# The last weight transfer of a mixer and mixture-of-experts block, divided by partitions

## The reference, cut to what matters

```python
x = x + mixed @ w_o                          # the two gated mixers, before the experts
h = rms_norm(x, norm_ffn)
combine = top_2_of_the_best_group(h)         # (256, 32), two weights per row, the rest zero
for e in range(32):
    a = silu(h @ w_gate[e]) * (h @ w_up[e])  # w_gate, w_up: (1024, 512) for each expert
    x = x + combine[:, e:e + 1] * (a @ w_down[e])   # w_down: (512, 1024)
out = rms_norm(x, norm_final)
```

## Time and profile before

| what | value |
|---|---|
| median of 3 runs | 729.03 us (728.8 to 730.17) |
| profiled execution, its own time | 728.23 us |
| its span, first to last instruction | 726.3 us |
| mean granted TensorE clock | 0.893 of full speed |
| mean rate of all transfers over the span | 334 GB/s |
| last unit (half 1): from its issue to its landing | 19.34 us |
| last unit: size | 1024 KB |

### The profile page before, as it was taken

The page is one execution under the profiler, slowest core; times in us unless marked ns, Lnnn a source line. Parts: engine busy times, 40 slices in busy tenths (PEclk is TensorE's granted clock), DMA queues, the critical chain, the costliest instruction groups (busy, mean ns, idle before and its releaser), DMA issues.

```text
span 726.3 us, 7579 instructions
## 1 busy us (share of the span) xinstructions
PE 554.2 (76%) x3257; PEld 331.3 (46%) x3257; DVE 204.1 (28%) x432; ACT 72.6 (10%) x139; POOL 43.9 (6%) x68
## 2 busy tenths in 40 slices
PE   6999999999999998998384594566448347457765
PEld 6888888888886656354041141123114113112411
DVE  3898979897012144000010000000001001000002
ACT  3101020202100013100000000000000000000002
POOL 5001212212000011000000000000000000000000
PEclk9999999999999999999696788779679669778988
DMA  9992812445495648899999999999999999999993
GB/s 248 390 304 83 292 56 71 161 157 192 144 406 232 231 174 319 354 431 428 427 426 430 428 426 430 429 427 426 431 425 427 430 429 427 427 429 426 424 406 152
DMA packets 46097, 242.43 MB, mean 334 GB/s; under 512 B 9618, under 2 KB 9710, under 8 KB 35822
## 3 DMA queue, kind: packets, MB, share of 16 engines
q1 hardware_dynamic: 45198, 238.77, 81.2%
q10 hardware_dynamic: 864, 3.15, 1.3%
HBM read 240.86 MB, written 1.05 MB: 333 GB/s over the span
## 4 chain that ended last, share of the span: by engine, by line
PE 52%; DMA 42%; DVE 2%; SPq 2%; issue 2%; ACT 0%; POOL 0%; DVEq 0%; PEldq 0%; POOLq 0%; ACTq 0%
PE bank L1150 29%; DMA ring<-in_w_down 15%; DMA ring<-in_w_gate 13%; PE bank L1389 8%; DMA s_region<-in_w_up 4%; DMA x_region<-in_w_up 4%; PE bank L1397 4%; DMA ring<-in_w_up 4%; PE bank L1271 4%; PE bank L1438 2%; DMA ring<-in_w_in 1%; SPq L471 1%; PE bank L1356 1%; PE bank L1243 1%; PE bank L1258 1%
## 5 line engine op out<-in xcount | busy, mean ns | idle before, releaser
L1389 PE MATMUL bank<-ring,z_region 128*32 128x512 f32 x688 | 116.3, 668 | 64.0 <-DMA ring<-in_w_gate 14.9
L1150 PE MATMUL bank<-x_region,ring 128*128 128x256 f32 x688 | 152.9, 381 | 0.0
L1150 PEld LDWEIGHTS bank<-x_region,ring 128*128 128x128 f32 x688 | 129.3, 190 | 22.5 <-issue 4.3
L1389 PEld LDWEIGHTS bank<-ring,z_region 128*32 128x32 f32 x688 | 32.8, 121 | 123.5 <-issue 123.5
L1397 PE MATMUL bank<-ring,m_region 128*32 128x512 f32 x240 | 55.4, 737 | 27.8 <-DMA ring<-in_w_down 16.6
L1063 DVE TENSOR_TENSOR z_region<-z_region,bank 128x512 f32<-128x512 f32 x8 | 8.2, 1027 | 209.3 <-PE bank L1389 197.2
L1389 PE MATMUL bank<-x_region,z_region 128*32 128x512 f32 x80 | 43.7, 708 | 11.0 <-DMA ring<-in_w_up 11.0
L1067 DVE COPY m_region<-bank 128x512 f32<-128x512 f32 x8 | 5.5, 692 | 141.7 <-PE bank L1397 113.6
L1397 PE MATMUL bank<-s_region,m_region 128*32 128x512 f32 x64 | 37.3, 750 | 9.0 <-DMA ring<-in_w_down 9.0
L1389 PE MATMUL bank<-rot_region,z_region 128*32 128x512 f32 x64 | 36.0, 727 | 8.4 <-DMA ring<-in_w_up 8.4
L1356 PE MATMUL bank<-conv_region,h_region 128*128 128x128 f32 x256 | 33.2, 285 | 4.7 <-issue 4.1
(11 more groups left out here) (244 smaller groups left out, 551.7 us busy)
## 6 DMA issues: line engine op xcount, KB each, us to landing
ring<-in_w_gate SPq DMA_DIRECT2D x29, 2048.0 KB, 34.5
ring<-in_w_up SPq DMA_DIRECT2D x20, 2048.0 KB, 32.4
ring<-in_w_down SPq DMA_DIRECT2D x20, 2048.0 KB, 35.2
ring<-in_w_in SPq DMA_DIRECT2D x11, 2048.0 KB, 10.3
s_region<-in_w_up SPq DMA_DIRECT2D x4, 2048.0 KB, 34.5
rot_region<-in_w_down SPq DMA_DIRECT2D x4, 2048.0 KB, 32.6
s_region<-in_w_down SPq DMA_DIRECT2D x4, 2048.0 KB, 35.9
x_region<-in_w_up SPq DMA_DIRECT2D x4, 2048.0 KB, 37.0
```

Source lines behind the costliest of these rows:

```text
L1150: ins = MM(dst, w[:, k, n * P:(n + 1) * P], rhs[:, k, :], start=k == 0, stop=k == kn - 1)
L1389: ins = MM(bank[to][quarter(e), :], xT[:, k, quarter(e)], of_expert[e][:, FF * k:FF * k + FF], start=k == 0, stop=k == KD - 1)
```

## The change

The last unit is issued as 16 DMAs. Each of them moves the 4 pieces of 2 KB for 8 neighbouring partitions, 64 KB in all. They go out one after the other on the SP queue and raise the same semaphore, so TensorE waits for 15 x 16 more. The other units are issued as before. The bytes, their source and their destination are the same.

```diff
+STRIP = 8
...
-                sp.dma_start(dst[:, 0:e * n].rearrange("p (e n) -> p e n", e=e), src).then_inc(landed, 16)
+                if v < len(UNITS) - 1:
+                    sp.dma_start(dst[:, 0:e * n].rearrange("p (e n) -> p e n", e=e), src).then_inc(landed, 16)
+                    return
+                for p in range(0, P, STRIP):
+                    sp.dma_start(dst[p:p + STRIP, 0:e * n].rearrange("p (e n) -> p e n", e=e),
+                                 src[p:p + STRIP]).then_inc(landed, 16)
...
                 uses = transfers_to(slot, range(MIX_UNITS)) + sum(slot_of(w) == slot for w in range(v + 1))
+                if v == len(UNITS) - 1:
+                    uses += P // STRIP - 1
                 pe.wait_ge(slots[slot][1], uses * 16)
```

## The result

The changed kernel takes 734.52 us (median of 9, 731.51 to 736.38) against 729.07 us (9 runs) for the kernel before: a ratio of 1.0073, 95% interval 1.0056 to 1.0090. It is slower by 5.4 us, and its times scatter over 4.9 us where these nine of the kernel before lie within 1.6 us (in a later set of 23 the kernel before scatters over 4.3 us, with one time above 731). The profiled execution took 732.92 us, 1.6 us less than the median, with a span of 730.8 us, 4.5 us longer than before.

The account below looks back on a forecast made before the run. The weights' arrival by DMA was taken to bound the kernel. Eight engines carrying the last unit (2.53 us) plus completions (0.1) made 2.63 us, added to 729.03 for 731.7 us, range 728.7 to 736.5.

Parts of the forecast that it names:

- the count of completions: Last unit's DMAs: completions rise from 16 to 128, small packets by 112; cost taken 0.1 us, at most 0.3.
- the mechanism that I called the likeliest: Last unit runs on eight engines, some of them late, with no slowdown between neighbouring partitions: 731.7 us, chance 0.36.
- my own signs of being wrong: Profile after: 16 completions per small transfer, rate below 150 GB/s, last landing still 715.7, or line 1479's matmuls at half clock.
- the blocking rival: Last unit: engines writing neighbouring partitions share a way into SBUF; 5.1 to 7.6 us more, 734.5 (732 to 740), chance 0.30.
- The end follows the data: End of kernel: each microsecond the last unit lands later adds one to the span; landing earlier gains 0.25 us at most.
- Half 0: Unit ahead of the divided one: goes first in every engine's queue, so its matmuls still start at 712.60 us.
- Eight engines: Last unit: a transfer of 8 partitions runs on eight engines, all 16 on the same eight; 5.07 us at 207 GB/s.
- A late engine among the eight, 2.53 us: Last unit: the eight engines used include some that finish late, so the end moves by 2.53 us; lower bound nothing.
- No blocking between neighbours: Last unit: engines writing neighbouring partitions do not slow each other; cost taken as nothing.
- Sixteen issues cost nothing: SP queue: 16 issues take 5.0 to 8.8 us, done by 710.2, needed about 717; cost nothing, cover 7 us.
- Slow sequence of small transfers: Last unit: the 16 transfers come out one per 1.5 us, ending 10 us late; 739 us, chance 0.07.
- TensorE's clock: TensorE at the end: a 2.9 us wait is too short to lower its clock; cost nothing, at most 1.5 us.

Follow-up runs that it names:

- warm matmuls: Against the changed kernel, unused matmuls added before TensorE's waits for half 0 (8) and for the copy of half 0 (2): 734.22 us, ratio 1.0064.

## Why the prediction was right, and where it was not

The direction, the range (728.7 to 736.5) and the count of completions were right. The point, 731.7 us, was 2.8 us too low, and the mechanism that I called the likeliest is only a part of what the runs show. Two of my own signs of being wrong came true: the rate fell below 150 GB/s (143 from 714 to 716 us), and half 1's matmuls ran in part at half clock (1.57 us against 1.07). The range held the result because it took in most of the blocking rival.

- *The end follows the data.* Right, but in the profile after the chain goes through half 0, which I had left where it was: "Half 0. It goes before the strips in every engine's queue; its matmuls start at 712.60 and should stay there." This is the step that failed. It holds for one engine's queue; between engines, an early engine's transfers slowed an earlier unit of a late one. Measured: half 0's matmuls start 3.36 us later, 1.83 of them spent waiting for data where it was 0.70 before. With 32 neighbours even the unit ahead of half 0 was waited for by 4.03 us.
- *Eight engines.* Shown by 112 more small packets.
- *A late engine among the eight, 2.53 us.* I took this against the bound of nothing, and it held. With partitions 4 apart the last 2 KB packet ends at 717.34 us against 714.85 before, 2.5 us later, with two engines' 49 GB/s at the end. Some six of the eight are early (60 completions against 18 between 708 and 711 us), and their share fell into their idle time, but the end follows the last engine. What was missing is what comes on top: in the changed kernel the last 2 KB packet ends at 718.85 us, 4.0 us later than before, and at 720.26 us in the profile with warm matmuls, 5.4 us later.
- *No blocking between neighbours.* I took the value nothing and priced blocking as a rival at 734.5 with a chance of 0.30. The measured median is 734.52, and 63 GB/s for 8 neighbours against 160 for partitions 4 apart, alone, shows that the grouping of partitions makes such transfers slow. That the price fits to 0.02 us is luck: the rival counted only a longer transfer of the divided unit, by 5.1 to 7.6 us, and neither half 0's delay nor the clock was in it. The rule in the Trainium skill, SBUF — State Buffer, section "Door 1: The DMA port swizzle", holds here in its form: spans of 8, 16, 32 and 64 neighbours moved 63, 121, 212 and 210 GB/s, and by its table they reach 2, 4, 8 and 8 ports. The last pair, the same rate for twice the partitions, is its most particular claim. An estimate from its 27.2 GB/s per port is 54 for 8 neighbours, where 63 were measured; transfers that follow each other reach different ports, and some overlap of them may be the reason. This agreement, and no run, is what puts the blocking on the side of SBUF and not of HBM. The late engines' slower packets while the strips went into low partitions are not explained by it.
- *Sixteen issues cost nothing.* Right for neighbours: 0.30 us each where SP did not wait for room, and the last went out at 708.12 us. With a step the issues take 0.68 us.
- *Slow sequence of small transfers.* Ruled out as the main cause: 8 transfers of 16 and 4 of 32 lose as much as 16 of 8, 2 of 64 lose 4.5 us, and 4 of 128 lose nothing.
- *TensorE's clock.* I took nothing, because the wait would be shorter than the 4.5 us of the earlier trace rows, and named 1.5 us as the most. That inference failed: TensorE waited 1.83 us, ran the matmuls of half 0, waited 0.72 us, and had half clock (0.50) from 717.7 on. The first addition took 2.08 us instead of 1.13; the extra between the two matmul groups is 1.14 us in all. Keeping the clock up in one place gave back nothing that could be told from the scatter, so its share is not settled.

Three things stay open. By what way the late engines are slowed from the first strip on. Why 32 neighbours are the slowest, when alone they move more than 8 or 16 do: its profile shows a wait of 4.03 us for the unit ahead of half 0, but not why that unit is held back more. And why the changed kernel scatters over 4.9 us: the lag between early and late engines when the divided unit comes up may differ between executions, which no run isolates. No divided version beat the kernel before. The transfers of all 128 partitions equal it, and it has only the 0.25 us that TensorE waited to give.

## What to carry to other kernels

If a load has to be divided, divide it along the free dimension and let each transfer span all 128 partitions (729.12 us here, no loss). Every division by partitions made the kernel slower, and alone, runs of 8, 16 and 32 neighbours moved 63, 121 and 212 GB/s. A DMA share near 1 is no proof of a full rate: read the GB/s beside it. And when transfers of different shapes follow each other on a queue, ask what the engines that are ahead do to those that are behind: the unit that is late can be one in front of the one you changed.

## What the runs showed of the hardware that I had not expected

- With one transfer shape per run and nothing beside it, 2.1 MB in 4 KB pieces moved at 350 to 362 GB/s into 128 partitions, 210 to 212 into 64 or 32 neighbours, 121 into 16 and 63 into 8; into 8 partitions 2 apart 112, 4 apart 160.
- An issue on SP of a transfer whose partitions have a step took 0.68 us, one of neighbouring partitions 0.30 us:

```profile
710.46 0.68 SPq L478 DMA_DIRECT2D ring<-in_w_down  x1
```

- Engines run some 3 us apart at the end of 400 us of steady loading, though every weight unit before the change gives each of them the same number of bytes. The packet records of the kernel before say where the lag comes from. The 16 completions of one unit lie within 1.7 us at 298 us and within 4.5 us at 685 to 689 us, in two groups of eight. From 311 to 686 us there are 16 packets of 16 KB on the queue that the page calls "q8 instruction", each of about 1 us, and with each of them one engine's completions move back by 1.3 to 1.6 us against the others and stay there. So nearly all of the lag, in which the early engines met the late ones, comes with the loading of instructions.
